# S5 by token group in steps beside the other group's SwiGLU, its weight-only tables made beside the first SwiGLU

## What is computed

```python
x = layer_norm(ALPHA * x + 0.5 * swiglu(x, ffn1))      # (silu(x @ w_gate) * (x @ w_up)) @ w_down
x = layer_norm(ALPHA * x + mix(x))
x = layer_norm(ALPHA * x + 0.5 * swiglu(x, ffn2))

def s5_layer(x):                                       # layer 1's mix: 64 groups x 16 channels, 64 complex states each
    lam_bar = exp(lam * dt);  b_bar = ((lam_bar - 1) / lam) * b
    s[t] = lam_bar * s[t-1] + b_bar @ u[t]             # along the tokens, from 0 (prompt) or a given state (samples)
    y[t] = real(c @ s[t]) + d_skip * u[t]
    g = gelu(y)
    return (g @ w_out) * sigmoid(g @ w_gate), s[last]
```

## Time and profile before

| | |
|---|---|
| median of 3 runs | 2738.49 us (2734.43 to 2738.73) |
| profiled execution | 2735.0 us, its span 2733.3 us |
| instructions in the span | 43046 |
| busy: PE | 2436.1 us, 89% |
| busy: DVE | 1707.0 us, 62% |
| busy: ACT | 998.7 us, 37% |
| busy: POOL | 496.3 us, 18% |
| DMA | 383.55 MB, mean 140 GB/s |

### The profile page before, as it was taken

One profiled execution on the slowest core, in us unless ns is written; L12 is line 12 of the kernel. 1 busy time (PEld: TensorE's weight loads), 2 busy tenths in 40 slices (PEclk: granted clock), 3 DMA queues, 4 the chain that ended last, 5 costly groups with the idle time before them and its releaser, 6 DMA issues. The chain is left out here.

```text
span 2733.3 us, 43046 instructions
## 1 busy us (share of the span) xinstructions
PE 2436.1 (89%) x17245; PEld 2287.8 (84%) x17245; DVE 1707.0 (62%) x2660; ACT 998.7 (37%) x1486; POOL 496.3 (18%) x559
## 2 busy tenths in 40 slices
PE   7999999989989999999999989994408799999996
PEld 7999989988876677988999989993306798999995
DVE  6666665666644556767555676555894467667554
ACT  3434443334432334424333344332203344434332
POOL 0711100033000122012100132005910022103003
PEclk9999999999999999989999999997557899999997
DMA  7665554344466865445555545541003555665452
GB/s 182 180 176 159 176 171 129 113 120 135 125 186 212 253 182 136 141 111 149 167 147 151 149 138 157 147 131 20 1 4 47 124 148 153 181 178 159 146 151 77
DMA packets 658616, 383.55 MB, mean 140 GB/s; under 512 B 29842, under 2 KB 629778, under 8 KB 658418
## 3 DMA queue, kind: packets, MB, share of 16 engines
q1 hardware_dynamic: 651890, 360.42, 46.6%
q0 software_dynamic: 6528, 20.37, 2.5%
HBM read 370.35 MB, written 6.19 MB: 138 GB/s over the span
## 5 line engine op out<-in xcount | busy, mean ns | idle before, releaser
L217 DVE TENSOR_TENSOR w_lo<-w_raw,w_hi 128x1024 fp32r<-128x1024 f32 (+1 forms) x648 | 801.5, 1240 | 593.8 <-ACT w_hi L208 592.2
L222 PE MATMUL ps<-x_hi,w_hi 128*128 128x256 f32 (+1 forms) x3200 | 962.4, 301 | 29.1 <-DVE w_lo L217 27.7
L223 PE MATMUL ps<-x_lo,w_hi 128*128 128x256 f32 (+1 forms) x3200 | 951.9, 297 | 0.0
L224 PE MATMUL ps<-x_hi,w_lo 128*128 128x256 f32 (+1 forms) x3200 | 951.3, 297 | 0.0
L208 ACT ACTIVATE w_hi<-w_raw 128x1024 fp32r<-128x1024 f32 (+1 forms) x648 | 668.8, 1034 | 623.1 <-PE ps L224 524.5
L222 PEld LDWEIGHTS ps<-x_hi,w_hi 128*128 128x128 f32 x3200 | 611.7, 191 | 42.8 <-DVE w_lo L217 30.8
L223 PEld LDWEIGHTS ps<-x_lo,w_hi 128*128 128x128 f32 x3200 | 612.1, 191 | 1.1 <-issue 0.2
L224 PEld LDWEIGHTS ps<-x_hi,w_lo 128*128 128x128 f32 x3200 | 611.6, 191 | 0.0
L222 PE MATMUL ps<-h_hi,w_hi 128*128 128x256 f32 (+1 forms) x1408 | 423.0, 300 | 11.7 <-DVE w_lo L217 10.7
L224 PE MATMUL ps<-h_hi,w_lo 128*128 128x256 f32 (+1 forms) x1408 | 417.4, 296 | 0.0
L223 PE MATMUL ps<-h_lo,w_hi 128*128 128x256 f32 (+1 forms) x1408 | 416.6, 296 | 0.0
(11 more groups left out here) (277 smaller groups left out, 2319.5 us busy)
## 6 DMA issues: line engine op xcount, KB each, us to landing
w_raw<-in_ffn_w_gate SPq DMA_DIRECT2D x176, 512.0 KB, 3.9
w_raw<-in_ffn_w_up SPq DMA_DIRECT2D x176, 512.0 KB, 3.9
w_raw<-in_ffn_w_down SPq DMA_DIRECT2D x128, 512.0 KB, 4.1
w_raw<-in_w_in_ab SPq DMA_DIRECT2D x56, 512.0 KB, 3.8
w_raw<-in_ffn_w_down SPq DMA_DIRECT2D x64, 384.0 KB, 3.4
arena<-in_cache_v POOLq DMA_DIRECT2D x64, 256.0 KB, 4.5
arena<-in_cache_k SPq DMA_DIRECT2D x64, 256.0 KB, 3.9
w_raw<-in_w_out_ab SPq DMA_DIRECT2D x16, 512.0 KB, 4.0
```

The costliest lines, as they stand in the source:

```text
L217: dve.tensor_tensor(T.w_lo[:, u % RING, 0:n], T.w_raw[:, u % RAW, 0:n], T.w_hi[:, u % RING, 0:n].bitcast(F32), ALU.subtract).then_inc(T.w_ ...
L222: pe.matmul(out, w_hi, m_hi, start=first, stop=False)
L223: pe.matmul(out, w_hi, m_lo, start=False, stop=False)
L224: return pe.matmul(out, w_lo, m_hi, start=False, stop=last)
```

## The change

One block instead of five. `first_layer` becomes `layers` and holds everything to the last store; `phase_s5_inputs`, `phase_s5_scan`, `phase_s5_outputs` and `dense_last` go.

`S5Prepare` (52 steps) does what rests on weights alone: B and C loaded by SP after the tables; `b_bar`, the powers of B (on DVE before) and C times powers on POOL; the turns and the kernel on PE; and three tables of 4 MB each stored by SP to DRAM (`made_rows`, `made_decays`, `made_taps`), octet by octet (8 of them, one each four steps). It is the side work beside f0a and f0b[:1], from SwiGLU step 9 or 10 on. The layer's input projection on ACT waits until all is stored, since both use the same memory. The loads of the S5 constants go ahead of those of B's tokens.

`S5Group` (11 steps of inputs, 12 of scan, 17 of outputs) does one group's tokens: it turns them octet by octet, loads the rows, taps and decays from DRAM (12 MB per group), and scans 32 chunks in 4 runs. Half of the scan's last part (`fix`) is POOL's. A starts from zero and stands beside f1b, one step per SwiGLU step from step 4; B starts from A's end state, has the sample tokens too, and stands beside f3a[:2], its inputs one per step, its scan and outputs two per step. The order of SwiGLUs is: f2a[1:], f1b with N3A and S5 of A, Out of A with N2B, f2b with N4A, f3a[:2] with N3B and S5 of B, Out of B, f3a[2:] with N4B, f3b with N5A.

The gate of Out uses Tanh(0.5 x) in place of Sigmoid, with the factor two taken up by the residual and the norm's epsilon.

```diff
+def woven(main, side):
+    for _ in main:
+        next(side, None)
+        yield
+    for _ in side:
+        yield
...
+def paced(steps, alone):
+    held = False
+    for i, _ in enumerate(steps):
+        held = not held and i not in alone
+        if not held:
+            yield
+    if held:
+        yield
 
...
-            act.activation(T.gate[:, d % 2, 0:g.n], T.ps[:, T.banks[o], 0:g.n], ACT.Sigmoid).then_inc(T.silu_done.h, 1)
+            act.activation(T.gate[:, d % 2, 0:g.n], T.ps[:, T.banks[o], 0:g.n], ACT.Tanh, scale=0.5)\
+               .then_inc(T.silu_done.h, 1)
...
-        dve.scalar_tensor_tensor(T.x[:, d, g.cols], T.x[:, d, g.cols], ALPHA, y, ALU.mult, ALU.add)\
+        dve.scalar_tensor_tensor(T.x[:, d, g.cols], T.x[:, d, g.cols], 2.0 * ALPHA if R.gated else ALPHA, y, ALU.mult,
+                                 ALU.add)\
...
+class S5Prepare:
...
+    FIRST, EVERY = 18, 4
+    STEPS = FIRST + EVERY * (KT - 1) + 6
+    TURN_C = 10
...
+        S = self.S
+        for i in range(self.STEPS):
+            q = self.at(i, 3)
+            if q is not None:
+                sp.wait_ge(S.b_moved.h, q + 1)
+                sp.dma_start(S.made_rows[q], self.b_rows[q % 2]).then_inc(S.rows_stored.h, 16)
+            q = self.at(i, 5)
+            if q is not None:
+                sp.wait_ge(S.c_done.h, q + 1)
+                decays = S.made_decays[q].rearrange("p (a s n) -> p a s n", a=A4, s=2)
+                for s in range(2):
+                    for r in range(2):
+                        sp.dma_start(decays[HALF[r], :, s],
+                                     self.c_pow[q % 2][HALF[s], r, :, 1:CL + 1, :].rearrange("p a k h -> p a (k h)"))\
+                          .then_inc(S.decays_stored.h, 16)
+                sp.wait_ge(S.placed.h, q + 1)
+                for t in range(CL):
+                    sp.dma_start(S.made_taps[q][t * GH:(t + 1) * GH].rearrange("p (i n) -> p i n", i=GT),
+                                 self.kernel[q % 2][0:GH, :, P - t * GH:2 * P - t * GH]).then_inc(S.taps_stored.h, 16)
+            yield
...
+            if i == self.TURN_C:
+                dve.wait_ge(S.sized.h, 1)
+                dve.reciprocal(S.size2[:, :], S.size2[:, :])
+                for t in range(CL):
+                    last = dve.tensor_copy(self.falling[:, :, t], S.powers[:, :, CL - 1 - t])
...
+                for a in range(A4):
+                    for r in range(2):
+                        for s in range(2):
+                            mm = pe.matmul(T.ps[0:GH, 6 + s, a * P:(a + 1) * P], self.b_bar[HALF[s], r, A4 * q + a, :],
+                                           self.c_pow[q % 2][HALF[s], r, a, 0:CL, :].rearrange("p k h -> p (k h)"),
+                                           start=(r == 0), stop=(r == 1))
+                mm.then_inc(S.tapped.h, 1)
...
+        def form_b(q, r):
+            if r == 0 and q >= 2:
+                pool.wait_ge(S.b_turned.h, q - 1)
+            a = slice(A4 * q, A4 * (q + 1))
+            wide = [P, A4, CL, GH]
+            b = [self.b_bar[:, r_, a, :].unsqueeze(2).to_broadcast(wide) for r_ in range(2)]
+            f = [self.falling[:, r_, :, a].rearrange("p t a -> p a t").unsqueeze(3).to_broadcast(wide) for r_ in range(2)]
+            out, m = self.b_pow[q % 2][:, r], self.m[:, :, 0:CL, :]
+            x, y, o = ((f[0], f[1], ALU.subtract), (f[1], f[0], ALU.add))[r]
+            pool.tensor_tensor(out, b[0], x, ALU.mult)
+            tt(m, b[1], y, ALU.mult)
+            tt(out, out, m, o)
+            if r:
...
+            for lag, form, r in ((-8, form_b, 0), (-7, form_b, 1), (-6, form_c, 0), (-5, form_c, 1)):
+                q = self.at(i, lag)
+                if q is not None:
+                    form(q, r)
...
+class S5Group:
...
+    INPUTS, SCAN = KT + 3, 12
+    OUTPUTS = 2 * KT + 1
+    STEPS = INPUTS + SCAN + OUTPUTS
...
+            sp.dma_start(self.taps[e % 2], S.made_taps[e].rearrange("p (i n) -> p i n", i=GT))\
+              .then_inc(S.spread[e % 2].h, 16)
+            sp.dma_start(self.decays[e % 2], S.made_decays[e].rearrange("p (i n) -> p i n", i=GT))\
+              .then_inc(S.spread[e % 2].h, 16)
...
+                for a in range(A4):
+                    for r in range(2):
+                        for s in range(2):
+                            mm = pe.matmul(T.ps[HALF[s], 7, (r * A4 + a) * c:(r * A4 + a + 1) * c],
+                                           self.b_rows[e % 2][:, r, a, HALF[s]], self.u[:, 2 * (A4 * e + a) + s, :],
+                                           start=True, stop=True)
+                mm.then_inc(S.added.h, 1)
...
+                for t in range(CL):
+                    for s in range(2):
+                        rows = slice(s * HD, s * HD + c)
+                        mm = pe.matmul(T.ps[HALF[s], 6 + (e - 1) % 2, t * c:(t + 1) * c],
+                                       self.gel[(e - 1) % 2][rows, t].rearrange("p a h -> p (a h)"),
+                                       T.ident[rows, rows], start=True, stop=True)
+                mm.then_inc(S.turned.h, 1)
...
+                for k in range(A4):
+                    for w in range(2):
+                        for s in range(2):
+                            j = s * A4 + k
+                            lhs, rhs = ((self.u[:, GT * e + j, :], self.taps[e % 2][:, j, :]),
+                                        (self.starts[e % 2][:, j, :], self.decays[e % 2][:, j, :]))[w]
+                            mm = pe.matmul(T.ps[s * HD:s * HD + c, 4 + s, k * P:(k + 1) * P], lhs, rhs,
+                                           start=(w == 0), stop=(w == 1))
+                mm.then_inc(S.mixed.h, 1)
...
+        wide = [P, GPAIRS, RUNS]
+        for j in range(1, RUN - 1):
+            advance([runs[:, r, :, :, j + 1] for r in range(2)], [runs[:, r, :, :, j] for r in range(2)], 0, wide)
+            yield
+        wide, flat = [P, GPAIRS, RUNS - 1], [P, GPAIRS]
+        advance([runs[:, r, :, 1:, 0] for r in range(2)], [runs[:, r, :, 0:RUNS - 1, RUN - 1] for r in range(2)], 0, wide)
+        end = [self.end[:, r] for r in range(2)]
+        advance(end, [runs[:, r, :, RUNS - 1, RUN - 1] for r in range(2)], 0, flat)
+        yield
+        for b in range(1 if self.before is None else 0, RUNS):
+            out = [runs[:, r, :, b + 1, 0] for r in range(2)] if b + 1 < RUNS else end
+            advance(out, [runs[:, r, :, b, 0] for r in range(2)], RUN - 1, flat)
+            if b == 1:
+                yield
+        dve.memset(self.part[:, 1023:1024], 0.0).then_inc(S.carried.h, 1)
+        yield
+        for a0 in (0, self.FIX):
+            self.fix(dve, T.dve_chain, self.part, a0)
+            yield
+        if self.before is not None:
...
+            if i == self.INPUTS + 8:
+                pool.wait_ge(S.carried.h, self.n + 1)
+                for a0 in (2 * self.FIX, 3 * self.FIX):
+                    self.fix(pool, T.pool_chain, self.part_pool, a0)
+                pool.memset(self.part_pool[:, 1023:1024], 0.0).then_inc(S.fixed_p.h, 1)
...
+        made = ((S.rows_stored, 16 * KT), (S.decays_stored, 64 * KT), (S.taps_stored, 16 * CL * KT))
+        PA = Project(T, M, A, w_in, range(SECTIONS), M.by, N0A.ready, made)
...
+        def norm_and_s5(norm, s5):
+            return together(norm, after(idle(Norm.STEPS - 2), s5))
+        def beside_a(norm, s5):
+            return paced(norm_and_s5(norm, s5), range(Norm.STEPS - 2, Norm.STEPS - 2 + S5Group.STEPS))
+        def beside_b(norm, s5):
+            first = Norm.STEPS - 2
+            return paced(norm_and_s5(norm, s5), range(first, first + S5Group.INPUTS))
...
+            weave(after(ffn(ffn_tensor, pe, f0a), woven(ffn(ffn_tensor, pe, f0b[:1]), N0A.tensor(pe))),
+                  after(S5C.tensor(pe), after(load_tensor(T, pe, B, rows, turned[B]), prepare.tensor(pe))))
...
-            run(ffn(ffn_tensor, pe, f1b))
-            weave(ffn(ffn_tensor, pe, f2a[2:]), N2B.tensor(pe))
-            weave(ffn(ffn_tensor, pe, f2b), N3A.tensor(pe))
-            run(N3B.tensor(pe))
+            weave(ffn(ffn_tensor, pe, f2a[1:]), N1B.tensor(pe))
+            weave(ffn(ffn_tensor, pe, f1b), beside_a(N3A.tensor(pe), s5_a.tensor(pe)))
+            weave(out_tensor(T, pe, OA2), N2B.tensor(pe))
+            weave(ffn(ffn_tensor, pe, f2b), N4A.tensor(pe))
+            weave(ffn(ffn_tensor, pe, f3a[:2]), beside_b(N3B.tensor(pe), s5_b.tensor(pe)))
+            run(out_tensor(T, pe, OB2))
+            weave(ffn(ffn_tensor, pe, f3a[2:]), N4B.tensor(pe))
+            weave(ffn(ffn_tensor, pe, f3b), after(N5A.tensor(pe), store_columns(pe, A)))
+            run(after(N5B.tensor(pe), store_columns(pe, B)))
```

More of the change, by code:

```diff
@@ L94, in weave, with together @@
         pass
+def woven(main, side):
[4 more added lines that the diff above has]
+        yield
+def together(first, second):
+    going = True
+    while going:
+        going = False
+        for steps in (first, second):
+            for _ in steps:
```

(5 more changed lines are left out.)

1106 lines of the change are left out of this document (553 added, 553 removed).

## The result

The median went from 2736.64 us to 2663.93 (2662.27 to 2670.38, 4 runs each): a ratio of 0.974, 95% interval 0.972 to 0.976, so 73 us faster where 110 were forecast. The profiled execution has a span of 2660.6 us, 72.7 less than before.

What follows compares the result with a forecast made beforehand. PE bounds the kernel, except in S5's stretch, a chain round DVE, POOL, ACT and PE. Span 2733.3 - 303.7 + 6 + (40 + 10) + (40 + 45) + 52 = 2622.6; forecast 2626 us, range 2555 to 2700.

Steps and rivals of the forecast that it cites:

- 1, the gap: End of norm N3B and the three S5 phases: the whole stretch without a SwiGLU goes, -303.7 us.
- 2, norms and borders: Norms beside SwiGLUs at their new places cost 44 us where the old stages lost 38: +6.
- 3, PE: S5's transposes, increments, mix and turn matmuls inside the SwiGLUs: 40 us of PE per group (31 to 55).
- 4, S5 of A: Beside group B's SwiGLU: waits, mainly at the two fix steps, +10 us (0 to 15) on top of PE's 40.
- 5, S5 of B: Beside group A's SwiGLU: +45 us on top of PE's 40, 35 for DVE's paired scan, 10 for loads and clock.
- 6, preparation: Beside the first SwiGLU: +52 us; PE work 24, stores 6, PE's wait for N0A's sums 20, clock 2.
- the term of the stores: In the preparation: SP's 13 issues per octet and 12 MB written beside weight loads, +6 us (0 to 20).
- (b): Rival: contention is worse, preparation at 95 us and B's S5 at 130; about 2710 us, chance 0.21.
- (a): Rival: DVE's scan and POOL's forms hide, so 10, 35 and 20 us go; about 2560 us, chance 0.20.
- (c): Rival: S5's 2120 records inside SwiGLUs cost 0.20 us each, 424 in all; about 2895 us, chance 0.06.
- (d): Rival: S5 does not overlap, PE sits out each of its 80 steps, about 100 us more; 2725 us, chance 0.05.
- The table loads: ACT alternating Gelu and SwiGLU gate: 12 loads of 1.28 us, 15 us, costed at nothing; by the skill about 9 more.

Runs made afterwards that it cites:

- the missing fix: Kernel with the third buffer and preparation four SwiGLU steps earlier, without the scan's last part (fix) on DVE and POOL in both groups: 2602.72 us.
- the other pairing: Kernel with the third buffer and preparation four SwiGLU steps earlier; S5 of B has inputs two per SwiGLU step and scan one per step: 2619.24 us.
- thin forms: Kernel with the third buffer, each of POOL's 32 forms (powers of B, C times powers) cut from three operations to one: 2608.11 us.
- the third buffer: Changed kernel with three buffers in place of two for C times powers, so POOL's octet q waits for the store of octet q-3: 2633.93 us.
- SP's order: Changed kernel, still two buffers, with SP storing an octet's decays four SwiGLU steps sooner: 2637.67 us.

## Why the prediction was right, and where it was not

- **1, the gap.** Right: the next SwiGLU runs on without a break, and the clock's long dip went with it.
- **2, norms and borders.** +1 where +6 stood. Out of A beside N2B with f2b behind lost 7 and 4 (52.8 from 1750.8 to 1803.6 against 45.7, and 236.4 from there to 2040.0 against 232.3) rather than 16; f3a[2:] beside N4B, from 2319.0 to 2384.0, lost 13.6, near the 15 of fa.
- **3, PE.** Right in size, with one line off: the five lines of A sum to 47.3 us for 40. The mix was right; increments and turns came at 9.0 each, the upper end, so fewer columns made the records no shorter than those of 72 columns; the u transposes took 5.4, above the range, 0.084 a record of 32 columns where one of 72 took 0.066.
- **4, S5 of A.** PE's extra 7 and a smaller stall (7.2 by the missing fix, forecast 10) cancel in part: 51 for 50, and luck has a share in that. f1b was to last about 285 and lasts 286.0. The path was another too: PE waits 1.8 us for w_lo, where the prediction looked for the stall, and 3.7 at the first mix, for an ACT copy that waits for the end of the fix.
- **5, S5 of B.** 82 for 85, but of other parts. PE's lines of S5 and its waits from 2040.0 to 2262.8:

```profile
L2192 PE MATMUL ps<-arena 128*40 128x128 f32 x256 | 17.3, 293 | 5.2 <-ACT arena L2230 5.2
...
PE ps L255 <- DVE w_lo L250: 16.3, 6, 5.0
```

  S5's lines sum to 51 us on PE, where 40 stood. PE waits 16.3 for w_lo behind the scan and 5.2 at the first mix, for ACT's copy of what the scan leaves: 21.5, where 35 stood. The remaining 9 are the SwiGLU's own matmuls at a lower clock (0.94 in the mean); the +10 for the clock and the loads of taps and decays comes to that, and no wait of PE at the mix for these loads is seen. The 11 too few and the 13.5 too many cancel: luck. DVE's prices hold: 2.7 us an advance, 1.3 a flat one, 3.7 the sample ends (forecast 4.5), 6.7 and 5.2 for the fixes that were put at 7.75. That DVE's paired scan stalls PE is shown twice, by the missing fix (15.0) and by the other pairing (8.2); its size was put too high. The check value given for this stage, 212, was a slip of addition: it took 1056 matmuls for 1152; 137 + 85 is 222, and 222.8 was measured.
- **6, preparation.** This is the step that failed: 97.5 for 52. Its PE work (24 forecast; the three lines sum to 26) and the size of POOL's pace (22 forecast, 26 by thin forms) hold. PE's wait for N0A's sums, 21.6 where some 20 were forecast, is right by luck: half of it was the loop's, as it fell to 10.0 with the third buffer. Mis-sized is the term of the stores, +6 with ends 0 and 20. It looked at one direction only, stores that hold up weight loads behind them in SP's queue. The other direction decides: weight loads hold up the stores, POOL's `decays_stored` wait hangs on them, and POOL's queue has N0A's sums behind it. The loop costs 30 (third buffer) or 27 (SP's order). The late stores at the projection cost another 7.6 (90.0 for 82.4), put at nothing, at most 5. Summed by the windows: 26 are PE's work, 25.7 go with the third buffer (485.8 to 460.1), another 27.2 with thin forms (371.3 to 344.1, the projection's start), and 6.4 of the late taps are left with the third buffer (88.8 for 82.4). That is 85 of the 97.5; some 12 stay open. In them is a weight load that landed late just behind the loads of B and C (ACT idles 10.1 us for it until 62.7, PE 6.9), which was not tried apart.
- **Rivals.** (b) had the right number for the preparation, 95, by the wrong mechanism: it named issues that hold back weight loads and write traffic, and both together are worth 5 beyond the loop (the late weight load at 62.7 apart, which is of this kind); its third part, POOL that waits for each w_lo, is in the 26 of the thin forms. Its other half, 130 for B, is refuted by 82. (a), (c) and (d) are refuted: stalls did not hide, S5's records cost 0.05 us each on PE (47.3 over 896), and in the waits of f1b and f3a[:2] PE stands for an ACT copy of S5 once per group, at the first mix (3.7 and 5.2 us).
- **The table loads.** Twelve were costed at nothing. There is one in each group. The timeline of ACT in f3a[:2] after, with the SwiGLU's gate (L401) and S5's Gelu (L2268):

```profile
2201.65 1.05 ACT L241 ACTIVATE w_hi<-w_raw 128x1024 fp32r<-128x1024 f32 x1
2202.71 1.28 ACT L2268 ACT_TABLE_LOAD   x1
2204.18 1.21 ACT L2268 ACTIVATE arena<-ps 40x512 f32<-40x512 f32 x2 [0.18 <-PE ps L2192]
...
2208.61 0.38 ACT L401 ACTIVATE gate<-ps 128x256 f32<-128x256 f32 x1 [0.95 <-PE ps L257]
...
2214.43 1.21 ACT L2268 ACTIVATE arena<-ps 40x512 f32<-40x512 f32 x2 [1.12 <-PE ps L2192]
```

The load at 2202.71 is the only one of S5's outputs; the gate and the Gelu alternate from then on without. From the end of the rounding at 2202.70 to the start of the Gelu are 1.48 us, of which 1.28 is the load; at A's first Gelu it is 1.31 (1649.18 to 1650.49). The Trainium skill (ScalarE: Activation LUTs, section What ACT_TABLE_LOAD costs) gives 2.66 for a switch with its drain; here no more than 1.48 is to be seen, and the 9 us that the forecast would have added by it did not come.

## What to carry to other kernels

When a step is moved beside other work, write down for each wait it brings where in the *program order* of the queue the event stands that ends it, and what is ahead of that event there. If the engine that waits is ahead of the engine that signals, count the buffers until it no longer is, or move the signal: here a store that frees a buffer had to stand before the loads of later steps. And where two engines slow each other (DVE and POOL here), do not expect a gain from giving work of one to the other: here it lost 5.5 us in the stretch, while less work gained 27.

## What was not expected of the hardware

- Gelu in its tanh form and the gate's Tanh run without a table load between them: 1 load for 8 Gelu steps and the gates between (above).
- DVE's operations grow by POOL's presence over a whole stage: with 42 of POOL's operations less in f0a (178 for 220), the same 224 instructions of DVE took 156.35 us in place of 182.58. The growth is in those that read two operands from SBUF (w_lo of 1024 elements 1.60 for 1.35 us in the mean, the h_lo of L426 0.85 for 0.68); those with one operand in PSUM did not grow (L416 0.41, L420 0.42 in both).
- Matmuls of 32 to 40 columns on half or a quarter of the array took 0.035 us a record (9.0 us for 256), as much as 72 columns took by halving the 2.24 us for 32 records, at a granted clock of 0.50, of the earlier trace rows: fewer columns did not make them cheaper.
